# The gate matrix of two feed-forward blocks, by seven products of 2x2 blocks instead of eight

## The chip, the cores and the metric

One NeuronCore of a Trainium2 chip runs the whole program. The metric is the device time of one execution in microseconds (us), the median of several runs. Engines are named as the profile names them: PE is TensorE (PEld its weight loads), DVE is VectorE, ACT is ScalarE, POOL is GpSimd, SP is SyncE, which here only issues DMAs.

## The reference

Two transformer layers over 512 tokens and 1024 features, in fp32. The first has a feed-forward block ahead of its mixer and one behind it, the second has one behind its mixer and its memory attention: three blocks in all, which the kernel numbers f = 0, 1, 2. Each of them computes

```
y = rmsnorm(x, g)                       # 512 x 1024
a = y @ w_gate;  b = y @ w_up           # each 512 x 2816  (in blocks 0 and 1: the halves of one w_in)
x = x + h * ((silu(a) * b) @ w_out)     # h = 0.5 for blocks 0 and 1, 1 for block 2
```

Everything else (sparse attention, convolution, memory attention, gated linear attention) lies between the blocks and is not touched here.

## The kernel before, in words

**Layout.** Features lie on the 128 partitions and tokens along the columns, so an activation is a set of tiles of 128 features x 512 tokens. The 2816 features of `a` and `b` are 22 rows of 128; a block takes them in two halves (h = 0, 1) of 11 (m = 0 to 10), and after each half it multiplies the 11 gated rows by `w_out` (`ffo`) into the residual `XT`.

**fp32 in three passes.** A number is split into a rounded high part and a low part (the rest). Each product is high x high, high x low and low x high, three matmuls that add up in one PSUM bank (`three`, with its matmul at L1135). So one row of `a` (`ffa`) or of `b` (`ffb`) is 8 slices of the 1024 input features x 3 passes = 24 matmuls of 128 x 128 weights on 512 columns (`dense`).

**Weights.** A unit is one row's weights: 128 x 1024 numbers, 512 KB. SP loads it into one of four buffers `raw` as soon as PE has finished the unit four before it; ACT copies it to one of three buffers `whi` as soon as PE has finished the unit three before it (`split` in `act_program`, L1677); DVE subtracts that copy from the raw numbers and writes the low part over them (`split` in `dve_program`, L2115). PE waits for both parts of a unit before its first matmul.

**Order.** There is one list of work items. Every engine walks through it in order and takes the items that concern it, so each engine's program is a fixed sequence, and an instruction that waits holds up all that follow on its engine. The low and high parts of unit u + 2 are put ahead of the DVE and ACT work of the item that uses unit u. In blocks 1 and 2 the list is in the order in which `ffn` writes it:

```
ffa m, ffb m, ffg m,   ffa m+1, ffb m+1, ffg m+1, ...
```

**The gate.** `ffg` of a row is, on DVE: the bank of `ffa` times the row of rsqrt factors `RB` (L2243), a wait for ACT's silu, the bank of `ffb` times `RB` (L2243), the product of the two (L2251), a wait for ACT's copy of the high part, the low part (L2120). The factor 1/rms is applied here, after the matmuls: the operand of the matmuls (`XH`, `XL`) is x times the gain only. The factors come late: `nstat` and `nspread` sum the squares and spread the result over the partitions with PE while PE already works on the first rows, and `RB` is copied out of a bank by DVE (L2223) just before the first `ffg`. In block 2 (f = 2) the first two rows wait for it, in block 1 the first.

**PSUM.** Eight banks; six of them (role `d`) form the ring from which `ffa`, `ffb` and `ffo` take theirs in turn.

Of the kernel before, what the change touches and what calls it, by code (L numbers as in the profile page):

```python
# [310 lines left out]
class Work:  # L311
# [3 lines left out]
    def __init__(self):  # L315
        self.items, self.units, self.heads, self.tiles = [], [], [], []
        self.merged = set()
        self.later = []
        self.spent = 0.0
        self.both = 0  # L320
# [80 lines left out]
def order():  # L401
# [4 lines left out]
    def ffn(f, ni, wa, wb, wo, oa, ob, nxt, jobs):  # L406
        late = []
        for h in range(2):
            for m in range(KF):
                first = h == 0 and m == 0  # L410
                if first and ni in EACH:
                    n, n2 = w.unit(wa, oa), w.unit(wb, ob)
                    w.both = 1
                    w.add_units("pair", (f,), [n, n2])
                    for k in range(KD):
                        w.add("normsq", ni, k)
                    w.both = 0
                    late = [one("ffg", f, h, 0)]
                    continue
# [12 lines left out]
                w.add("ffg", f, h, m)  # L432
                if f == 0 and h == 0 and m == 3:
                    w.add("rel")
                if f == 0 and (m in (4, 7, 10) if h == 0 else m in (1, 4, 7)):
                    w.add("table_out", tables.pop(0))
                if h:
                    w.step(jobs)
            for m in range(KD):
                a = w.unit(wo, h * KD + m, 6 * P)  # L440
                b = w.unit(wo, h * KD + m, 5 * P, 6 * P)
                w.add_units("ffo", (f, h, m), [a, b])
                if f == 0 and h == 0 and m in (2, 5):
# [491 lines left out]
def build(nc, A, out):  # L935
# [158 lines left out]
    full = signal("bank_full")  # L1094
    w_hi, w_lo = signal("weight_hi"), signal("weight_lo")
    x_hi, x_lo = signal("operand_hi"), signal("operand_lo")
# [33 lines left out]
    def pe_program(e):  # L1130
# [162 lines left out]
        def ffo(f, h, m, n, n2):  # L1293
            dense(("ffo", f, h, m), n, GH, GL, ("g", f, h), nk=6, last=False)
            dense(("ffo", f, h, m), n2, GH, GL, ("g", f, h), nk=5, k0=6, first=False)

        def conv(m, part, n):
# [354 lines left out]
        def mmo(m, n, k):  # L1652
# [9 lines left out]
        do = dict(banks=set_banks, nstat=nstat, nspread=nspread, memstat=memstat, warm=warm, start=start, pair=pair, ffa=ffa, ffb=ffb, ffo=ffo, conv=conv,  # L1662
                  convg=convg, wide=wide, widestat=widestat, widefin=widefin, memv=memv, mgate=mgate, score=score,
# [9 lines left out]
    def act_program(e):  # L1673
        on = Once(e)

        def copy(o, i, **how):
            return e.activation(o, i, ACT.Copy, **how)  # L1677

        def split(n):
            width = unit[n][2]  # L1680
            on.wait_ge(*d_raw[n % NRAW].at(n))
            on.wait_ge(*full.at(("u", n - NHI)))
# [68 lines left out]
        def memnorm(i, k):  # L1751
# [4 lines left out]
            if k >= 3:  # L1756
                on.wait_ge(*calc.at(("macc", i, k - 2)))
            e.activation(a[1 + k % 2] if k else a[0], x, ACT.Square).then_inc(*curve.tick(("msq", i, k)))

        def ffg(f, h, m):  # L1760
# [323 lines left out]
        def relload():  # L2084
# [3 lines left out]
        e.dma_start(vec, A["vec"]).then_inc(*d_vec.tick(0, by=16))  # L2088
        do = dict(gain=gain, nspread=nspread, start=start, relload=relload, norm=norm, normsq=normsq, memload=memload, memnorm=memnorm, ffg=ffg, convg=convg,
                  wide=wide, widefin=widefin, memvs=memvs, mgate=mgate, sgate=sgate,  # L2090
# [5 lines left out]
        for (kind, *args), upto in w.items:  # L2096
# [3 lines left out]
            if kind in do:  # L2100
                do[kind](*args)

    def dve_program(e):
        on = Once(e)
        parts = {}

        def split(n):
            name, _, width, _ = unit[n]
            on.wait_ge(*w_hi.at(n))
            if name in STACKED:  # L2110
# [130 lines left out]
        def times(o, item, done, free=True):  # L2241
            on.wait_ge(*full.at(item))
            e.tensor_tensor(o, banks[item], RB, ALU.mult).then_inc(*evac.tick(done, ("free", item)))  # L2243

        def ffg(f, h, m):
            a, s = T[2 * m % 4], T[2 * m % 4 + 1]
            times(a, ("ffa", f, h, m), ("ffat", f, h, m))
            on.wait_ge(*curve.at(("silu", f, h, m)))
# [507 lines left out]
        def final(k):  # L2756
            n = 2 if k < 6 else 1
            if k == 7:
# [7 lines left out]
        e.memset(ZER, 0.0).then_inc(*zeroed.tick("mem"))  # L2766
        do = dict(start=start, norm=norm, normsq=normsq, nstat=nstat, nspread=nspread, memnorm=memnorm, memstat=memstat, ffg=ffg, ffo=ffo, conv=conv, tap=tap, cmerge=cmerge,
                  convg=convg, widestat=widestat, widefin=widefin, memvs=memvs, mgate=mgate, sgate=sgate,
# [61 lines left out]
    def sp_program(e):  # L2830
        on = Once(e)

        def load(n):
            name, j, width, off = unit[n]
            on.wait_ge(*full.at(("u", n - NRAW)))
            if name == "w_gkv":
                h, c = j
                for k in range(2):
                    e.dma_start(raw[n % NRAW].rearrange("p (q k c) -> p q k c", q=4, k=2)[:, :, k, :],
                                A[name][4 * h:4 * h + 4, :, k * 384 + c * P:k * 384 + (c + 1) * P].rearrange("q p c -> p q c")).then_inc(  # L2840
                        *d_raw[n % NRAW].tick(n, by=16))
            else:
                e.dma_start(raw[n % NRAW][:, 0:width], A[name][j, :, off:off + width]).then_inc(*d_raw[n % NRAW].tick(n, by=16))
# [162 lines left out]
```

## Time and profile before

| | |
|---|---|
| Median of 3 runs | 2375.48 us (2374.09 to 2375.69) |
| The profiled execution: its own time | 2373.52 us |
| Its span, first to last instruction | 2371.6 us |
| Granted TensorE clock, mean over the span | 0.999 of full |
| Busy: PE / PEld / DVE / ACT / POOL | 2348.5 / 1966.2 / 1420.3 / 1000.3 / 164.6 us |
| Instructions on PE / DVE / ACT | 11448 / 2891 / 1852 |
| HBM read and written | 217.83 MB and 11.53 MB |

The busy time of an engine is the union of its instructions, so that overlapping matmuls count once. A duration in a row runs from an instruction's start to its recorded end; the next instruction may start a little before that end. In the timeline, "[x <-Y]" behind an instruction says that its engine sat idle for x us before it, until Y was done.

### The profile page before, as it was taken

The page shows a single profiled execution, that of the slowest core. Times are in us where ns is not written, and L with a number is a line of the kernel's source. Part 1 is how long each engine was busy: PE and PEld are TensorE (multiplying, and loading weights), DVE is VectorE, ACT ScalarE, POOL GpSimd, SP SyncE. Part 2 cuts the span into 40 slices and gives each one's busy share as a digit, 9 for nine tenths or more (in the row PEclk, how much of TensorE's full clock was granted, in tenths as well). Part 3 has the DMA queues.
Part 4 walks back from the last instruction along what each step waited for, and adds up shares of the span by engine and source line. Part 5 has one row for each costly group of instructions (what it writes and reads, how often), then busy time and mean ns, then how long its engine had stood idle before and what let it go on. Part 6 is the DMA issues. An engine that isn't in the chain of part 4 may idle for free.

```text
span 2371.6 us, 30179 instructions
## 1 busy us (share of the span) xinstructions
PE 2348.5 (99%) x11448; PEld 1966.2 (83%) x11448; DVE 1420.3 (60%) x2891; ACT 1000.3 (42%) x1852; POOL 164.6 (7%) x250
## 2 busy tenths in 40 slices
PE   9999999999999999999999999999999999999998
PEld 7888889888888888878888888888888887888887
DVE  6434546674658897875434446677754667543444
ACT  5223335442335686653322334666523446322322
POOL 0000000110001223310000000111100001000000
PEclk9999999999999999999999999999999999999999
DMA  4455434332332211223333333212123432223322
GB/s 151 117 119 141 118 112 148 116 107 81 116 102 80 72 54 63 67 90 97 98 90 110 98 108 115 81 55 62 63 80 116 134 106 66 95 89 108 98 88 90
DMA packets 86409, 231.33 MB, mean 98 GB/s; under 512 B 8504, under 2 KB 23480, under 8 KB 86266
## 3 DMA queue, kind: packets, MB, share of 16 engines
q1 hardware_dynamic: 81072, 221.42, 29.4%
q10 hardware_dynamic: 5194, 7.98, 2.1%
q8 instruction: 93, 1.52, 0.3%
q14 instruction: 50, 0.41, 0.1%
HBM read 217.83 MB, written 11.53 MB: 97 GB/s over the span
## 4 chain that ended last, share of the span: by engine, by line
PE 96%; DVE 2%; ACT 1%; issue 1%; POOL 0%; DVEq 0%; ACTq 0%
PE bank L1135 93%; PE bank L1384 2%; PE bank L1210 1%; PE bank L1558 0%; PE bank L1231 0%; DVE t_pw L2387 0%; DVE t_pp L2387 0%; DVE t_PS L2120 0%; DVE t_wlo L2115 0%; ACT t_whi L1677 0%; ACT t_pw L1830 0%; DVE t_XT L2763 0%; DVE t_XL L2124 0%; POOL t_pw L2797 0%; DVE t_PW L2120 0%
## 5 line engine op out<-in xcount | busy, mean ns | idle before, releaser
L1135 PE MATMUL bank<-t_XH,t_whi 128*128 128x512 f32 x2064 | 812.0, 393 | 0.5 <-DVE t_wlo L2115 0.5
L1135 PE MATMUL bank<-t_XL,t_whi 128*128 128x512 f32 x2064 | 803.6, 389 | 0.0
L1135 PE MATMUL bank<-t_XH,t_wlo 128*128 128x512 f32 x2048 | 798.0, 390 | 0.0
L2115 DVE TENSOR_TENSOR t_wlo<-t_raw,t_whi 128x1024 fp32r<-128x1024 f32 (+2 forms) x416 | 478.5, 1152 | 385.8 <-ACT t_whi L1677 382.1
L1677 ACT ACTIVATE t_whi<-t_raw 128x1024 fp32r<-128x1024 f32 (+3 forms) x422 | 416.9, 989 | 436.5 <-PE bank L1135 373.4
L1135 PEld LDWEIGHTS bank<-t_XH,t_whi 128*128 128x128 f32 x2064 | 387.6, 188 | 81.6 <-issue 2.2
L1135 PEld LDWEIGHTS bank<-t_XL,t_whi 128*128 128x128 f32 x2064 | 387.8, 188 | 77.3
L1135 PEld LDWEIGHTS bank<-t_XH,t_wlo 128*128 128x128 f32 x2048 | 384.4, 188 | 81.0
L1135 PE MATMUL bank<-t_RX,t_whi 128*128 128x512 f32 x1056 | 325.1, 389 | 0.0
L2243 DVE TENSOR_TENSOR t_tmp<-bank,t_RB 128x512 f32<-128x512 f32 x178 | 122.5, 688 | 198.3 <-PE bank L1135 193.0
L1135 PEld LDWEIGHTS bank<-t_RX,t_whi 128*128 128x128 f32 x1056 | 198.2, 188 | 41.2
L1135 PE MATMUL bank<-t_RX,t_wlo 128*128 128x512 f32 x528 | 205.4, 389 | 0.0
L1677 ACT ACTIVATE t_RX<-t_tmp 128x512 fp32r<-128x512 f32 x66 | 41.7, 632 | 209.2 <-DVE t_tmp L2251 209.2
L1135 PEld LDWEIGHTS bank<-t_RX,t_wlo 128*128 128x128 f32 x528 | 99.1, 188 | 20.6
L2794 POOL TENSOR_SCALAR t_pp<-t_pp,t_sa,t_gn 128x512 f32<-128x512 f32 (+3 forms) x128 | 88.1, 694 | 335.5 <-DVE t_sa L2400 335.0
L1830 ACT ACTIVATE t_pp<-t_pp,t_sa 128x256 f32<-128x256 f32 (+3 forms) x144 | 79.6, 555 | 52.7 <-DVE t_sa L2387 51.9
L2797 POOL TENSOR_SCALAR t_pw<-t_pw,t_sa,t_cst 128x256 f32<-128x256 f32 (+1 forms) x80 | 47.6, 599 | 726.0 <-DVE t_sa L2400 696.9
L1765 ACT ACTIVATE t_tmp<-t_tmp 128x512 f32<-128x512 f32 x66 | 41.7, 632 | 132.5 <-DVE t_tmp L2243 132.5
L1677 ACT ACTIVATE t_XH<-t_XT,t_vec 128x512 fp32r<-128x512 f32 x48 | 34.5, 724 | 108.1 <-DVE t_XT L2264 52.6
L1135 PE MATMUL bank<-t_OA,t_whi 128*128 128x512 f32 x256 | 79.3, 391 | 0.0
L2264 DVE SCALAR_TENSOR_TENSOR t_XT<-bank,t_XT 128x512 f32<-128x512 f32 x47 | 32.5, 691 | 74.1 <-PE bank L1135 74.1
L2120 DVE TENSOR_TENSOR t_RX<-t_tmp,t_RX 128x512 fp32r<-128x512 f32 x66 | 45.7, 693 | 46.0 <-ACT t_RX L1677 46.0
(334 smaller groups left out, 2678.4 us busy)
## 6 DMA issues: line engine op xcount, KB each, us to landing
t_raw<-in_f_in SPq DMA_DIRECT2D x86, 512.0 KB, 3.5
t_raw<-in_f_out SPq DMA_DIRECT2D x32, 384.0 KB, 3.1
t_raw<-in_w_conv SPq DMA_DIRECT2D x24, 512.0 KB, 3.5
t_raw<-in_w_merge SPq DMA_DIRECT2D x24, 512.0 KB, 3.4
t_raw<-in_fg SPq DMA_DIRECT2D x22, 512.0 KB, 3.4
t_raw<-in_fu SPq DMA_DIRECT2D x22, 512.0 KB, 3.5
t_raw<-in_f_out SPq DMA_DIRECT2D x32, 320.0 KB, 3.0
t_raw<-in_w_g SPq DMA_DIRECT2D x16, 512.0 KB, 3.4
```

The costliest lines, as they stand in the source:

```text
L1135: return e.matmul(o, l, r, start=start, stop=stop, skip_group_check=True)
L1210: f = e.transpose(b[:, i * P:(i + 1) * P], r, ident)
L1384: f = e.transpose(b[:, j * P:(j + 1) * P], spare(hd, t)[:, j * P:(j + 1) * P], ident)
L1677: return e.activation(o, i, ACT.Copy, **how)
L1765: e.activation(s, a, ACT.Silu).then_inc(*curve.tick(("silu", f, h, m)))
L1830: e.activation(p, p, ACT.Exp, scale=-1.0, bias=s[:, 0:1], accum_out=s[:, 1:2]).then_inc(*curve.tick(("ex", t)))
L2115: e.tensor_tensor(wlo[n % NRAW][:, 0:width], raw[n % NRAW][:, 0:width], f32(whi[n % NHI][:, 0:width]), ALU.subtract).then_inc(*w_lo.tick(n))
L2120: e.tensor_tensor(o, x, f32(hi), ALU.subtract).then_inc(*x_lo.tick(item, *more))
L2243: e.tensor_tensor(o, banks[item], RB, ALU.mult).then_inc(*evac.tick(done, ("free", item)))
L2264: e.scalar_tensor_tensor(XT[:, m, :], banks[item], HALF[f], XT[:, m, :], ALU.mult, ALU.add).then_inc(*evac.tick(("free", item), *done))
L2794: e.tensor_scalar(p, p, r, gn[:, i, k:k + 1], ALU.mult, ALU.mult).then_inc(*scaled.tick(t))
L2797: e.tensor_scalar(p, p, r, cst[:, C_ONE:C_ONE + 1], ALU.mult, ALU.mult).then_inc(*scaled.tick(t))
```

## The change

In blocks 1 and 2, 15 of the 22 pairs of neighbouring feature rows of the gate matrix (rows m and m + 1) are computed together. Block 1 keeps its first five rows (`PLAIN`) and the last row of its second half as they were; block 2 keeps its first seven and the same last one. That leaves 3 + 5 pairs in block 1 and 2 + 5 in block 2. `ffb`, the up matrix, stays as it was.

For a pair, two rows x two slices of the input features give a 2 x 2 matrix of weight blocks (128 x 128 each), and the two slices x two halves of the tokens a 2 x 2 matrix of data blocks (128 x 256 each). Their product is formed from seven block products of sums of blocks instead of eight block products. There are four such steps for a pair (q = 0 to 3, two slices each), and the products add up over q in halves of four PSUM banks (`ffs`). Each product still takes three passes, so a pair is 4 x 7 x 3 = 84 matmuls of 256 columns in place of 48 matmuls of 512 columns.

- **Units.** A seven-product unit loads 512 of 1024 columns (256 KB, in runs of 1 KB); `add_up` on DVE forms the four sums of weight blocks beside them (three instructions: 256, 128 and 128 columns, each waiting for the one before). ACT then copies all 1024 columns, and DVE takes their low part, as for any unit.
- **Data.** `xna` on DVE multiplies two slices of x by gain and `RB` (two instructions of 512 columns) and forms four blocks of sums (four of 256); `xnb` splits the seven blocks: three copies on ACT (256, 512 and 1024 columns) and three subtractions on DVE. Four of each per feed-forward block, set between the first items that follow `nspread`.
- **Result.** `ffm` copies one product out on ACT (256 columns) and adds up the seven products on DVE in six instructions (five of 256 columns, one of 512) into the tiles in which `ffg` expects `a`; for these rows `ffg` leaves out its first multiplication by `RB`.
- **Order.** A pair's items are `ffs` q = 0, `ffb` m, `ffs` q = 1, 2, 3, `ffm`, `ffb` m + 1, `ffg` m, `ffg` m + 1: six units, of which four are of the new kind. On DVE, `add_up` of unit n + 1 stands ahead of the low part of unit n.

```
+                seven = f in PLAIN and (m >= PLAIN[f] if h == 0 else m < KF - 1)
+                if seven:
+                    def seven_unit(q):
+                        n = w.unit(wa, (oa + h * KF + m, q), 4 * P)
+                        w.seven.append(n)
+                        w.add_units("ffs", (f, h, m, q), [n])
+
+                    seven_unit(0)
+                    w.lin("ffb", f, h, m, name=wb, j=ob + h * KF + m)
+                    for q in range(1, KD // 2):
+                        seven_unit(q)
+                    w.add("ffm", f, h, m)
+                    w.lin("ffb", f, h, m + 1, name=wb, j=ob + h * KF + m + 1)
+                    w.add("ffg", f, h, m)
+                    w.add("ffg", f, h, m + 1)
+                    m += 2
                     continue
                 w.lin("ffa", f, h, m, name=wa, j=oa + h * KF + m)
...
+                if spread and forms:
+                    w.add(forms[0][0], f, forms.pop(0)[1])
                 w.lin("ffb", f, h, m, name=wb, j=ob + h * KF + m)
                 if first or late:
                     w.add("nspread", ni)
+                    spread = True
+                    if forms:
+                        w.add(forms[0][0], f, forms.pop(0)[1])
                 while late:
                     late.pop()()
...
                 w.add("ffg", f, h, m)
+                if spread and forms:
+                    w.add(forms[0][0], f, forms.pop(0)[1])
```

`forms` is the list xna 0, xna 1, xnb 0, xna 2, xnb 1, xna 3, xnb 2, xnb 3. On the engines, PE, the `split` of ACT, and DVE's walk through the list in turn:

```
+SEVEN = ((A1, X11, 0, 0), (ACD, T2, 0, 1), (AC, T3, 1, 0), (D_, T4, 3, 0), (CD, T1, 3, 1), (B, X21, 2, 0), (ABCD, X22, 2, 1))
...
+        def ffs(f, h, m, q, n):
+            if q == 0:
+                for z in range(4):
+                    take("d", ("ffs", f, h, m, z))
+            hi, lo = weights(n)
+            operand(("xn", f, q))
+            for wi, xi, z, half in SEVEN:
+                o = banks[("ffs", f, h, m, z)][:, 256 * half:256 * half + 256]
+                c, x = slice(wi * P, (wi + 1) * P), slice(256 * xi, 256 * xi + 256)
+                done = three(o, hi[:, c], lo[:, c], NH[q][:, x], NL[q][:, x], q == 0 and wi in (A1, AC, D_, B), q == 3)
...
+            on.wait_ge(*(w_sum if n in summands else d_raw[n % NRAW]).at(n))
...
-        n = 2
+        n, a = 2, 2
         for (kind, *args), upto in w.items:
             while n < min(upto - 1 + NHI, len(unit)):
+                while a < min(n + 2, upto + NHI, len(unit)):
+                    if a in summands:
+                        add_up(a)
+                    a += 1
                 split(n)
                 n += 1
+            while a < min(upto + NHI, len(unit)):
+                if a in summands:
+                    add_up(a)
+                a += 1
```

## Rows read from the trace of the kernel before

**Rows 1.** The page: busy time of each engine; the chain that ended last.
```profile
PE 2348.5 (99%) x11448; PEld 1966.2 (83%) x11448; DVE 1420.3 (60%) x2891; ACT 1000.3 (42%) x1852; POOL 164.6 (7%) x250
...
PE 96%; DVE 2%; ACT 1%; issue 1%; POOL 0%; DVEq 0%; ACTq 0%
```

**Rows 2.** Busy time by window, half 1 of block 1: PE, PEld, DVE, ACT, POOL, clock, DMA.
```profile
1270.00:1379.00 109.00, 109.00 (x482) 90.28 (x481) 51.53 (x62) 32.23 (x40) 0.00 (x0) 1.00 0.29 94
```

**Rows 3.** Timeline of that stretch: start, us, engine, line, operation, tiles.
```profile
1300.60 0.39 PE L1135 MATMUL bank<-t_XH,t_wlo 128*128 128x512 f32 x1
1300.82 0.39 PE L1135 MATMUL bank<-t_XH,t_whi 128*128 128x512 f32 x1
...
1301.01 22.09 SPq L2843 DMA_DIRECT2D t_raw<-in_f_in  x5
1301.08 1.06 ACT L1677 ACTIVATE t_whi<-t_raw 128x1024 fp32r<-128x1024 f32 x1 [2.39 <-PE bank L1135]
1302.17 1.23 DVE L2115 TENSOR_TENSOR t_wlo<-t_raw,t_whi 128x1024 fp32r<-128x1024 f32 x1 [2.23 <-ACT t_whi L1677]
1303.32 0.68 DVE L2243 TENSOR_TENSOR t_tmp<-bank,t_RB 128x512 f32<-128x512 f32 x1
...
1306.53 0.69 DVE L2243 TENSOR_TENSOR t_tmp<-bank,t_RB 128x512 f32<-128x512 f32 x1 [2.53 <-PE bank L1135]
1307.26 0.69 DVE L2251 TENSOR_TENSOR t_tmp<-t_tmp 128x512 f32<-128x512 f32 x1
1308.52 1.05 ACT L1677 ACTIVATE t_whi<-t_raw 128x1024 fp32r<-128x1024 f32 x1
1308.64 0.69 DVE L2120 TENSOR_TENSOR t_RX<-t_tmp,t_RX 128x512 fp32r<-128x512 f32 x1 [0.70 <-ACT t_RX L1677]
```

**Rows 4.** Window of eight slices on 256 columns: matmuls of the memory keys alone.
```profile
368.32:371.19 2.87, 2.87 (x24) 2.82 (x23) 0.00 (x0) 0.00 (x0) 1.00 0.57 153
```

**Rows 5.** Groups of VectorE instructions by shape: count, busy us, mean ns.
```profile
L2251 DVE TENSOR_TENSOR t_tmp<-t_tmp 128x512 f32<-128x512 f32 x66 | 45.7, 692 | 2.2
...
L2124 DVE SCALAR_TENSOR_TENSOR t_XL<-t_XT,t_vec,t_XH 128x512 fp32r<-128x512 f32 x48 | 35.7, 749 | 25.9 <-ACT t_XH L1677 25.5
...
L2120 DVE TENSOR_TENSOR t_PS<-bank,t_PS 128x256 fp32r<-128x256 f32 x32 | 13.3, 416 | 0.8 <-ACT t_PS L1677 0.6
...
L2120 DVE TENSOR_TENSOR t_PS<-bank,t_PS 128x128 fp32r<-128x128 f32 x32 | 9.1, 283 | 1.4 <-ACT t_PS L1677 1.2
```

**Rows 6.** DMA issues: KB each, median us from issue to landing.
```profile
t_raw<-in_f_in SPq DMA_DIRECT2D x86, 512.0 KB, 3.5
...
t_raw<-in_w_gkv SPq DMA_DIRECT2D x24, 256.0 KB, 3.0
...
t_XT<-x_kept SPq DMA_DIRECT2D x16, 256.0 KB, 2.7
...
out<-t_XT SPq DMA_DIRECT2D x8, 256.0 KB, 2.4
```

**Rows 7.** Timeline, start of block 2: VectorE behind the copy of `RB`, then PE.
```profile
2021.21 0.69 DVE L2243 TENSOR_TENSOR t_tmp<-bank,t_RB 128x512 f32<-128x512 f32 x1
...
2025.33 0.68 DVE L2243 TENSOR_TENSOR t_tmp<-bank,t_RB 128x512 f32<-128x512 f32 x1
...
2029.78 2.36 DVE L2115 TENSOR_TENSOR t_wlo<-t_raw,t_whi 128x1024 fp32r<-128x1024 f32 x2 [0.26 <-ACT t_whi L1677]
...
2030.97 0.39 PE L1135 MATMUL bank<-t_XH,t_wlo 128*128 128x512 f32 x1
2031.20 0.42 PE L1135 MATMUL bank<-t_XH,t_whi 128*128 128x512 f32 x1
```

**Rows 8.** Timeline of VectorE, start of block 1, behind the copy of `RB`.
```profile
1094.99 0.69 DVE L2243 TENSOR_TENSOR t_tmp<-bank,t_RB 128x512 f32<-128x512 f32 x1
...
1099.45 1.22 DVE L2115 TENSOR_TENSOR t_wlo<-t_raw,t_whi 128x1024 fp32r<-128x1024 f32 x1 [0.26 <-ACT t_whi L1677]
...
1105.25 0.69 DVE L2243 TENSOR_TENSOR t_tmp<-bank,t_RB 128x512 f32<-128x512 f32 x1 [2.53 <-PE bank L1135]
```

More of the change, by code:

```diff
@@ L90 @@
 NRAW = 4
+PLAIN = {1: 5, 2: 7}
+B, A1, D_, AC, CD, ACD, ABCD = 0, 1, 2, 4, 5, 6, 7
+X11, X21, X22, T1, T3, T2, T4 = range(7)
+SEVEN = ((A1, X11, 0, 0), (ACD, T2, 0, 1), (AC, T3, 1, 0), (D_, T4, 3, 0), (CD, T1, 3, 1), (B, X21, 2, 0), (ABCD, X22, 2, 1))
 class Signal:
@@ L317, in __init__ @@
         self.merged = set()
+        self.seven = []
         self.later = []
@@ L407, in ffn @@
         late = []
+        forms = [("xna", 0), ("xna", 1), ("xnb", 0), ("xna", 2), ("xnb", 1), ("xna", 3), ("xnb", 2), ("xnb", 3)] if f in PLAIN else []
+        spread = False
         for h in range(2):
-            for m in range(KF):
+            m = 0
+            while m < KF:
                 first = h == 0 and m == 0
@@ L432, in ffn @@
                 w.add("ffg", f, h, m)
+                if spread and forms:
+                    w.add(forms[0][0], f, forms.pop(0)[1])
+                    if h == 0 and f in PLAIN and m == PLAIN[f] - 1:
+                        while forms:
+                            w.add(forms[0][0], f, forms.pop(0)[1])
                 if f == 0 and h == 0 and m == 3:
@@ L1029, in build @@
     OM = [place(f"OM{q}", 12800 + q * 1024, 1024, F32R).rearrange("p (k n) -> p k n", k=2) for q in range(2)]
+    NAT = (17920, 21504, 25088, 3072)
+    NS = [place(f"ns{j}", NAT[j], 1792) for j in range(4)]
+    NL = [place(f"nl{j}", NAT[j], 1792, F32R) for j in range(4)]
+    NH = [place(f"nh{j}", NAT[j] + 1792, 1792, F32R) for j in range(4)]
+    TN = [[place(f"tn{d}{q}", (256, 1792)[d] + 512 * q, 512) for q in range(2)] for d in range(2)]
+    P1, U2, V2 = place("p1", 1280, 256), place("u2", 1536, 256), place("v2", 28672, 256)
     sa = [sb(f"sa{i}", [P, 8]) for i in range(RING)]
@@ L1660, in mmo @@
                 banks.let_go(("mmo", m))
-        do = dict(banks=set_banks, nstat=nstat, nspread=nspread, memstat=memstat, warm=warm, start=start, pair=pair, ffa=ffa, ffb=ffb, ffo=ffo, conv=conv,
+        do = dict(banks=set_banks, nstat=nstat, nspread=nspread, memstat=memstat, warm=warm, start=start, pair=pair, ffa=ffa, ffb=ffb, ffs=ffs, ffo=ffo, conv=conv,
                   convg=convg, wide=wide, widestat=widestat, widefin=widefin, memv=memv, mgate=mgate, score=score,
@@ L1679, in split @@
         def split(n):
-            width = unit[n][2]
-            on.wait_ge(*d_raw[n % NRAW].at(n))
+            width = UNIT if n in summands else unit[n][2]
+            on.wait_ge(*(w_sum if n in summands else d_raw[n % NRAW]).at(n))
             on.wait_ge(*full.at(("u", n - NHI)))
@@ L1758, in memnorm, with xnb, ffm @@
             e.activation(a[1 + k % 2] if k else a[0], x, ACT.Square).then_inc(*curve.tick(("msq", i, k)))
+        def xnb(f, j):
+            b, a = TN[j % 2]
+            on.wait_ge(*calc.at(("xn", f, j)))
+            copy(NH[j][:, 0:256], b[:, 0:256]).then_inc(*x_hi.tick(("xn0", f, j)))
+            copy(NH[j][:, 256:768], a).then_inc(*x_hi.tick(("xn0", f, j)))
+            on.wait_ge(*calc.at(("xns", f, j)))
+            copy(NH[j][:, 768:1792], NS[j][:, 768:1792]).then_inc(*x_hi.tick(("xn", f, j)))
+        def ffm(f, h, m):
+            on.wait_ge(*full.at(("ffs", f, h, m)))
+            if merged:
+                on.wait_ge(*evac.at(("ffat", *merged.pop())))
+            merged.append((f, h, m))
+            copy(P1, banks[("ffs", f, h, m, 0)][:, 0:256]).then_inc(*copied.tick(("p1", f, h, m)))
         def ffg(f, h, m):
@@ L2101, in act_program @@
                 do[kind](*args)
+    summands = set(w.seven)
     def dve_program(e):
@@ L2105, in dve_program @@
         parts = {}
+        sevens = set()
         def split(n):
             name, _, width, _ = unit[n]
+            width = UNIT if n in summands else width
             on.wait_ge(*w_hi.at(n))
@@ L2245, in ffg @@
         def ffg(f, h, m):
             a, s = T[2 * m % 4], T[2 * m % 4 + 1]
-            times(a, ("ffa", f, h, m), ("ffat", f, h, m))
+            if (f, h, m) not in sevens:
+                times(a, ("ffa", f, h, m), ("ffat", f, h, m))
             on.wait_ge(*curve.at(("silu", f, h, m)))
@@ L2841, in load @@
                         *d_raw[n % NRAW].tick(n, by=16))
+            elif n in summands:
+                row, q = j
+                e.dma_start(raw[n % NRAW][:, 0:width].rearrange("p (m c) -> p m c", m=2),
+                            A[name][row:row + 2, :, 256 * q:256 * q + 256].rearrange("m p c -> p m c")).then_inc(*d_raw[n % NRAW].tick(n, by=16))
             else:
```

58 lines of the change are left out of this document (54 added, 4 removed).

## The prediction

> **What bounds the kernel now.** Read the page first: PE is busy for 2348.5 of 2371.6 us, and the chain that ended last lies on it for 96% [rows 1]. Both say that only what shortens PE's own work, or makes PE wait, shows in the time. Then take the stage that is changed, by window: in the second half of block 1 PE has no gap in 109 us, while VectorE works for 51.5 and ScalarE for 32.2 [rows 2]. So in these stages whatever PE saves comes off the time as long as the weights arrive, and VectorE has some half of its time to give. Whether that is enough cannot be seen from the sum, since VectorE's order is fixed: the timeline is needed.
>
> In the timeline look at the clockwork of a unit. SyncE's five loads start 22.09 us apart from first start to last end; less one issue of 0.33 this makes four steps of 5.44 us [rows 3], one unit on PE: 24 matmuls, 0.227 us each. PE's end of a unit (its last matmul 1300.60 to 1300.99, the next unit's first at 1300.82) releases the load 0.19 us, and ScalarE 0.26 us, after that next unit has begun [rows 3]; VectorE I put at 0.27. A finished instruction releases another engine about 0.03 us later (ScalarE's copy ends at 1302.14, VectorE starts at 1302.17) [rows 3].
>
> **PE's own saving.** Memory keys show the new shape: three passes on 256 columns, 24 matmuls in 2.87 us, 0.1196 us each [rows 4]. That is more than half of 0.227, so seven products for eight do not save an eighth. A new unit has 7 x 3 = 21 matmuls, 2.51 us. A pair with its two up rows takes 2 x 5.44 + 4 x 2.51 = 20.92 us in place of 4 x 5.44 = 21.76: 0.84 us less, and 15 x 0.84 = 12.6 us if nothing waits.
>
> **VectorE's new work.** Prices: 128, 256 and 512 columns cost 283, 416 and 692 ns, two-step instructions of 512 columns 749 [rows 5]; 1024 columns 1.23 us, and the next independent instruction starts 1.15 us after it, 0.08 before its end, a dependent one 0.03 to 0.04 behind the end (1306.53 + 0.69, next 1307.26) [rows 3]. None of the sums is in the trace with its broadcast operand; I take the rows of the same width; for one of 256 columns the rows of 128 and 512 are the bounds, 0.28 and 0.69.
> - Sum step of a unit: 0.42 + 0.28 + 0.28 and two hand-offs, 0.97 us until the next may start.
> - Low part of a unit: 1.15.
> - Merge of a pair: five of 256 and one of 512 columns, two of them dependent: 2.41.
> - Gate of a row without its first multiplication: 0.73 + 0.72, ScalarE's copy with its hand-offs 0.70 [rows 3], then 0.61 to 0.65: 2.73. With the first multiplication and the wait for silu: 4.12 (2021.21 to 2025.33) [rows 7].
> - Data, first step: two of 749 and four of 256 columns: 2.90. Second step, with ScalarE's copies done: 256, 512 and 1024 columns, 2.10.
>
> Per pair this is 4 x 0.97 + 6 x 1.15 + 2.41 + 2 x 2.73 = 18.7 of PE's 20.9 us. It fits only if VectorE hardly ever waits.
>
> **Where VectorE waits.** Number a pair's units 0 to 5 (0, 2, 3, 4 are new, 1 and 5 the up rows), the next pair's from 6. VectorE's order around unit 5 is: sum of 6, low of 5, low of 6, merge, sum of 8, low of 7, two gates, sum of 9, low of 8. The sum of 6 waits for a load that SyncE starts when PE has finished unit 2, and the low part of unit 5 is queued behind it, though its own numbers are there. From PE's end of unit 2: 0.19 to the issue, the load's landing L, 0.03, the sum 0.97, the low part 1.23, and 0.19 to the first matmul (a low part that ended at 2031.01 met a matmul at 2031.20, so at most that) [rows 7]: L + 2.61. PE reaches unit 5 after two units, 5.02 us. So PE waits L - 2.41, and each pair that is followed by another gains 0.84 - (L - 2.41) = 3.25 - L.
>
> L is not shown for 256 KB in runs of 1 KB. The rows of that size: output stores 2.4, the spilled residual read back 2.7, a gated-attention weight in shorter runs 3.0; a full unit 3.5 [rows 6]. I take 3.0, the row nearest in kind (a strided weight load into the same buffers); bounds 2.4 and 3.5. Gain 0.25 each. There are 2 + 4 in block 1 and 1 + 4 in block 2: 11 x 0.25 = 2.75 us, between 9.2 (no wait) and -2.75. The last pair of each half has no such sum behind it and keeps 0.84: 4 x 0.84 = 3.36. Together 6.1 us.
>
> Is VectorE then on time for unit 8? From the sum of 6: 2.16 (low of 5; low of 6 waits for ScalarE) + 1.15 + 2.41 + 0.97 + 1.15 + 5.46 + 0.97 + 1.42 = 15.69 us. PE from the same point: 2.39 + 5.44 + 2.51 + 5.44 = 15.78. A draw; I count nothing, but any excess is paid on 11 pairs.
>
> **What the data steps cost.** They hide in VectorE's free time between plain rows only as long as a low part behind them is still early.
> - Block 2: before, the first low part behind the two late gates started at 2029.78, 0.33 us after VectorE was free (2025.33 + 4.12 = 2029.45), ended at 2031.01, and PE took it at 2031.20 without a break [rows 7]: no slack. Two first steps now stand ahead of it, one before the gates and one behind: 2 x 2.90 - 0.33 = 5.47 us of PE waiting.
> - Block 1: one late gate. The low part started at 1099.45, 0.34 after VectorE was free (1094.99 + 4.12). It now starts at 1099.11 + 5.80 = 1104.91 and frees PE at 1106.33; PE wants it at 1105.25 - 0.27 = 1104.98 [rows 8]. 1.35 us.
> - Then each pair of plain units carries a first and a second step: 1.15 + 2.10 + 1.15 + 4.12 + 2.90 = 11.42 us of VectorE for PE's 10.88. 0.54 us, twice in each block: 2.16.
> - Block 1 goes into its pairs with one plain row in between, VectorE still behind: the last second step, waiting 0.2 us for ScalarE, and the first sums cost 11.77 - 10.88 = 0.89 and 8.34 - 7.95 = 0.39: 1.28. Block 2 has two plain rows, enough to catch up.
>
> Sum 5.47 + 1.35 + 2.16 + 1.28 = 10.3 us. If the steps were hidden in full it would be 0; if every one of the eight were paid in both blocks, 2 x 4 x (2.90 + 2.10) = 40.
>
> **The sum.** 10.3 - 6.1 = 4.2 us slower. The profiled execution took 2373.5, which gives 2377.7; the median of the runs is 2.0 above it, so 2379.7 is forecast. ScalarE's added copies (some 9 of 21 us per pair in all) lie under VectorE's. Between L = 2.7 and 3.3 the forecast runs from 2376.4 to 2383.0.
>
> **Rivals.**
> 1. *VectorE becomes the bound of the pairs.* For it: the draw above, and that 18.7 of 20.9 us leave no room. Against: the low parts overlap by 0.08 us today [rows 3]. If the thirteen independent starts in the 15.69 us came only at the end of the one before, the chain grows by 1.04, PE waits 0.95 more per pair: 11 x 0.95 = 10.5, 2390. It decides from an excess of 0.1 us. The Trainium skill ("VectorE: DVE Perf Modes", section "The DRAIN you can't avoid") says that the next operation does not start until the pipe is empty. By that rule this rival holds; the trace agrees with it only for dependent instructions (1307.26) and shows 0.08 us of overlap for independent ones (1303.32).
> 2. *The load lands early, not slower.* At L = 2.4 the sum of 6 makes PE wait for nothing, 15 x 0.84 - 10.3 = 2.3 us faster, 2373.2; it is faster than before from L = 2.6 down. For it: stores of this size at 2.4. Against: no load from memory is under 2.7 [rows 6], and a full unit is in flight when this one starts.
> 3. *The data steps hide after all*, because the rows of the steps are shorter than I priced them or PE's wait there eats later slack: 6.1 us faster, 2369.4. Against: block 2's low part had no slack [rows 7], and nothing in VectorE's order can pass it.
> 4. *The change does not give PE its saving:* with four banks in turn, a matmul takes as long as its weight load, 24 loads of some 0.19 (188 to 192 ns) instead of 0.12. 84 x 0.19 = 16.0 for 10.0: 15 x 6.0 = 90 us slower, 2465 less what VectorE then no longer costs. Against: the loads overlap in the window of 256 columns [rows 4].
>
> **How the numbers follow.** Forecast 0.48, rivals 0.22, 0.18, 0.08, 0.04. About 0.2% (4.75 us) can be told from no change: faster is below 2370.7, slower above 2380.2. Of the forecast's 0.48, 2380.2 cuts off some 0.22; with rivals 1 and 4, slower 0.48. Same: the rest, 0.26, with 0.16 of rival 2: 0.42. Faster: 0.08 and 0.02. The range 2371 to 2391 leaves out rival 3, rival 4 and the end of rival 1, 0.18.
>
> **What would show it.** Windows in the pairs: 84 matmuls in 10.0 us. The chain and PE's waits: a wait of about 0.6 us for the low part at each unit 5, 11 times, with VectorE idle ahead of the sum of 6 until a load lands; one wait of some 5.5 us at the start of block 2 and one of 1.4 in block 1. Wrong would be: waits at unit 8 instead (rival 1), a landing of 2.4 (rival 2), no wait at block 2's start (rival 3), PE's steps of 0.19 us (rival 4).

## The result, and the profile after

The change makes the kernel slightly slower: 2381.66 us (median of 10 runs, 2379.03 to 2383.80) against 2375.35 (10 runs, 2374.09 to 2375.80). The ratio is 1.0027, 95% interval 1.0018 to 1.0035. The forecast was 2379.7, the range 2371 to 2391. The profiled execution took 2383.09 us (span 2381.3), near the top of its runs.

The page of the kernel after, which answers to [rows 1]: busy time by engine, and the chain.

```profile
PE 2345.0 (98%) x11988; PEld 1985.0 (83%) x11988; DVE 1561.5 (66%) x3233; ACT 1050.7 (44%) x1921; POOL 166.6 (7%) x250
...
PE 92%; DVE 5%; DMA 1%; ACT 1%; issue 1%; POOL 0%; DVEq 0%; SPq 0%; ACTq 0%
```

PE is busy for 3.5 us less, but VectorE and DMA now hold 6% of the chain, where VectorE held 2%: PE waits. The window of block 1's second half, against [rows 2], shows little of it there: VectorE's work has grown from 51.53 to 84.79 us, PE's idle time is 0.2 us. Idle time understates a wait: it is counted from the recorded end of PE's last matmul, which lies behind the start that the next one would have had. By the loads (below) the waits in this window come to some 1 us.

```profile
1270.00:1379.00 109.00, 108.79 (x664) 97.37 (x664) 84.79 (x145) 45.09 (x55) 0.00 (x0) 1.00 0.32 102
```

PE's waits by window (total, times, longest), first in block 1, then in block 2, show where it is:

```profile
PE bank L1178 <- DVE t_wlo L2190: 4.0, 6, 1.2
...
PE bank L1178 <- DVE t_wlo L2190: 8.9, 8, 5.3
```

All are waits for a low part. The longest, 5.3 us, is at the start of block 2. The timeline of VectorE there answers to [rows 7]:

```profile
2023.36 1.42 DVE L2336 SCALAR_TENSOR_TENSOR t_tn<-t_XT,t_vec,t_RB 128x512 f32<-128x512 f32 x2
...
2026.28 0.68 DVE L2318 TENSOR_TENSOR t_tmp<-bank,t_RB 128x512 f32<-128x512 f32 x1
...
2034.49 1.41 DVE L2336 SCALAR_TENSOR_TENSOR t_tn<-t_XT,t_vec,t_RB 128x512 f32<-128x512 f32 x2
...
2037.41 1.22 DVE L2190 TENSOR_TENSOR t_wlo<-t_raw,t_whi 128x1024 fp32r<-128x1024 f32 x1
```

```profile
2033.11 0.39 PE L1178 MATMUL bank<-t_XH,t_wlo 128*128 128x512 f32 x1
...
2038.77 0.77 PE L1178 MATMUL bank<-t_XH,t_whi 128*128 128x512 f32 x1 [5.27 <-DVE t_wlo L2190]
2039.33 0.63 PE L1178 MATMUL bank<-t_XL,t_whi 128*128 128x512 f32 x1
2039.76 0.63 PE L1178 MATMUL bank<-t_XH,t_wlo 128*128 128x512 f32 x1
```

The first data step takes 2026.28 - 2023.36 = 2.92 us and stands once ahead of the two gates and once (2034.49 to 2037.41) behind them; the low part that PE needs comes last. What PE does behind the gap is new: its matmuls start 0.43 us apart, not 0.23. The windows of that stretch (PE, PEld, DVE, ACT, POOL, granted clock, DMA share, GB/s) say why:

```profile
2028.00:2033.40 5.40, 5.40 (x25) 4.22 (x23) 3.72 (x6) 1.44 (x3) 0.00 (x0) 1.00 0.29 97
2033.50:2038.70 5.20, 0.00 (x0) 0.00 (x0) 4.75 (x9) 4.02 (x6) 0.00 (x0) 0.92 0.32 102
2038.70:2041.00 2.30, 2.23 (x5) 1.84 (x6) 2.30 (x4) 0.00 (x0) 0.00 (x0) 0.50 0.00 0
...
2043.00:2045.00 2.00, 2.00 (x6) 1.59 (x6) 1.38 (x2) 0.52 (x2) 0.00 (x0) 0.57 0.00 0
2045.00:2048.00 3.00, 3.00 (x14) 2.44 (x14) 2.71 (x6) 3.00 (x6) 0.00 (x0) 1.00 0.00 0
```

The granted clock is 1.00 (2.4 GHz) before the gap, 0.50 (1.2 GHz) for some 6 us behind it, and then 1.00 again. What gap and clock cost together is seen in two of SyncE's loads, each of which starts when PE ends a unit. They are 5.50 us apart before and 13.80 after, so 8.3 us are lost here:

```profile
2031.39 0.33 SPq L2843 DMA_DIRECT2D t_raw<-in_fu  x1
2036.89 0.33 SPq L2843 DMA_DIRECT2D t_raw<-in_fg  x1
```

```profile
2033.53 0.33 SPq L2980 DMA_DIRECT2D t_raw<-in_fu  x1
2047.33 0.33 SPq L2980 DMA_DIRECT2D t_raw<-in_fg  x1
```

Inside the pairs, too, the clockwork is best read from SyncE's loads, since a load starts when PE ends the unit four places earlier. From the first of the three loads of units 8 to 10 (one line, x3) to the load of unit 11 PE works on units 5, 6 and 7; without a wait that step takes 13.45 us, as e8 below shows. Second half of block 2:

```profile
2199.09 0.37 SPq L2977 DMA_DIRECT2D t_raw<-in_fg  x1
2201.61 0.34 SPq L2980 DMA_DIRECT2D t_raw<-in_fu  x1
2204.13 9.04 SPq L2977 DMA_DIRECT2D t_raw<-in_fg  x3
2218.27 0.34 SPq L2980 DMA_DIRECT2D t_raw<-in_fu  x1
```

```profile
2202.17 0.43 DVE L2324 TENSOR_TENSOR t_raw<-t_raw 128x256 f32<-128x256 f32 x1 [3.21 <-DMA t_raw<-in_fg]
...
2203.17 2.43 DVE L2190 TENSOR_TENSOR t_wlo<-t_raw,t_whi 128x1024 fp32r<-128x1024 f32 x2
```

The load of unit 6 starts at 2199.09; VectorE idles for 3.21 us until it lands, sums from 2202.17, and only then makes unit 5's low part. The step is 2218.27 - 2204.13 = 14.14: a wait of 0.69. Such steps stand at all 11 places; what they exceed 13.45 by is 0.17 to 1.08, 6.7 us in all. (The expectations of e1 and e5 count 7.7 for the same waits; by these steps it is 6.7.)

For each kernel below, the same four times were read from its profiled execution: the start of block 1's first load, from there to the first load behind block 1, from there to block 2's fifth load (its first four start well ahead of it, between the blocks), and from there to the end of the span.

| kernel | start | block 1 | between | block 2 | median, us | before, us |
|---|---|---|---|---|---|---|
| before | 1066.2 | 365.4 | 576.5 | 363.6 | | |
| after | 1067.5 | 366.3 | 576.4 | 371.1 | 2381.7 | 2375.4 |
| steps alone (e4) | 1068.2 | 367.8 | 576.2 | 371.1 | 2385.2 | 2375.0 |
| steps later (e2) | 1067.4 | 365.5 | 576.2 | 365.8 | 2376.9 | 2375.0 |
| filler (e3) | 1068.6 | 365.6 | 576.2 | 366.2 | 2377.5 | 2375.0 |
| every sum behind (e1) | 1068.7 | 373.2 | 576.2 | 373.3 | 2393.2 | 2375.0 |
| first sum behind (e5) | 1067.5 | 364.7 | 576.2 | 368.1 | 2380.1 | 2374.8 |
| first sum, steps later (e6) | 1068.0 | 368.6 | 576.3 | 365.2 | 2377.9 | 2374.8 |
| sums on GpSimd (e7) | 1069.4 | 363.8 | 576.6 | 366.8 | 2377.6 | 2374.8 |
| sums and subtractions on GpSimd (e8) | 1068.1 | 359.3 | 576.5 | 358.4 | 2364.5 | 2374.8 |
| 13 pairs (e9) | 1067.7 | 362.8 | 578.9 | 362.0 | 2374.2 | 2375.0 |
| sums on GpSimd, steps later (e10) | 1067.9 | 363.8 | 576.5 | 363.2 | 2373.5 | 2375.0 |

The start differs by up to 3 us ahead of any changed code, and e9 lost 2.4 us between the blocks in a wait that no edit touches; so the columns of the blocks say more of an edit than single times do.

### The profile page after: what moved, and what is told of

Read it like the earlier page. It is cut to its first block, busy times and chain, and to the rows that moved or that the text cites. A ratio compares the mean times of both kernels' runs of the same rounds, so it can differ in the third digit from the quotient of the medians.

```text
span 2381.3 us, 31773 instructions
## 1 busy us (share of the span) xinstructions
PE 2345.0 (98%) x11988; PEld 1985.0 (83%) x11988; DVE 1561.5 (66%) x3233; ACT 1050.7 (44%) x1921; POOL 166.6 (7%) x250
## 4 chain that ended last, share of the span: by engine, by line
PE 92%; DVE 5%; DMA 1%; ACT 1%; issue 1%; POOL 0%; DVEq 0%; SPq 0%; ACTq 0%
PE bank L1178 88%; PE bank L1439 2%; DVE t_wlo L2190 1%; DMA t_raw<-in_fg 1%; PE bank L1253 1%; DVE t_tmp L2318 0%; DVE t_tn L2336 0%; DMA t_raw<-in_f_in 0%; PE bank L1613 0%; DVE t_tmp L2376 0%; DMA t_XT<-in_xT 0%; PE bank L1274 0%; DVE t_nl L2195 0%; ACT t_RX L1733 0%; DVE t_pp L2512 0%
## 5 line engine op out<-in xcount | busy, mean ns | idle before, releaser
L1178 PE MATMUL bank<-t_XH,t_whi 128*128 128x512 f32 x1824 | 721.7, 396 | 12.4 <-DVE t_wlo L2190 11.3
L1178 PE MATMUL bank<-t_XL,t_whi 128*128 128x512 f32 x1824 | 711.8, 390 | 0.0
L1178 PE MATMUL bank<-t_XH,t_wlo 128*128 128x512 f32 x1808 | 705.8, 390 | 0.0
L1178 PEld LDWEIGHTS bank<-t_XH,t_whi 128*128 128x128 f32 x1824 | 343.4, 188 | 86.2 <-issue 15.8
L1178 PEld LDWEIGHTS bank<-t_XH,t_wlo 128*128 128x128 f32 x1808 | 340.1, 188 | 72.6
L1178 PEld LDWEIGHTS bank<-t_XL,t_whi 128*128 128x128 f32 x1824 | 343.7, 188 | 67.2
L1178 PE MATMUL bank<-t_nh,t_whi 128*128 128x256 f32 x420 | 119.0, 283 | 1.6 <-DVE t_wlo L2190 1.5
L1178 PE MATMUL bank<-t_nl,t_whi 128*128 128x256 f32 x420 | 118.8, 283 | 0.0
L1178 PE MATMUL bank<-t_nh,t_wlo 128*128 128x256 f32 x420 | 118.8, 283 | 0.0
L1178 PEld LDWEIGHTS bank<-t_nh,t_whi 128*128 128x128 f32 x420 | 80.5, 192 | 4.0 <-ACT t_whi L1733 1.8
```

The costliest lines, as they stand in the source:

```text
L1178: return e.matmul(o, l, r, start=start, stop=stop, skip_group_check=True)
```

## The experiments

**The start of block 2: steps alone, steps later, filler.** Is it the data steps that cost, and is the slow clock the gap's doing?

> The data steps alone, at the places of the kernel after; all 22 pairs of rows computed as before, so the forms that the steps make are read by nobody. Theory: 5.4 + 2.6 us at block 2's start, 1.2 at block 1's, 0.54 twice in block 1: 2375.4 + 10.3 = 2385.7 us. Rival (the steps hide, the loss is in the pairs): 2375.4 us. If the clock at block 2's start stays at 1.00: 2375.4 + 5.4 + 1.2 + 2.2 = 2384.2 us.

```
-                seven = f in PLAIN and (m >= PLAIN[f] if h == 0 else m < KF - 1)
+                seven = False
```

Measured: 2385.16 us, ratio 1.0043 (1.0030 to 1.0055). Block 1 is 2.4 us longer than before, block 2 7.5, together 9.9; the gap at block 2's start is the same 5.26 us. The steps by themselves cost nearly what was expected, without a pair in the kernel; the rival falls. The clock's part was smaller than expected: the step around the gap is 12.96 us here, 13.80 after.

> The kernel after, with the data steps moved: in block 2 none beside the two late gates, the first one a row later and then as before, two to a row, up to the last plain row; in block 1 none ahead of the late gate. The same work on every engine. Theory (the steps cost where a low part behind them has no slack, and block 2's gap of 5.3 us takes the clock down after it): block 2 gets back 5.4 us of waiting and 2.6 us of slow matmuls, block 1 some 2.5 us of waits; 2381.7 - 10.5 = 2371.2 us, with a granted clock of 1.00 at the start of block 2. Rival (the steps hide, the whole loss is in the pairs): 2381.7 us.

```
-                if spread and forms:
+                if spread and forms and m >= f:
...
                     spread = True
-                    if forms:
-                        w.add(forms[0][0], f, forms.pop(0)[1])
...
-                if spread and forms:
+                if spread and forms and m >= 3 * f - 3:
```

(The first place is between a row's two units, the second ahead of the late gates, the third behind a row's gate; the step that reuses a buffer also waits for VectorE's own last reading of it.) Measured: 2376.89 us, ratio 1.0009 (1.0000 to 1.0018): 4.8 us back, where 10.5 were expected. The waits at both starts are gone, but PE now waits where each block goes into its pairs. SyncE's loads there in block 2:

```profile
2070.76 10.22 SPq L2975 DMA_DIRECT2D t_raw<-in_fg  x3
2088.10 0.34 SPq L2978 DMA_DIRECT2D t_raw<-in_fu  x1
```

The step is 17.34 us where 13.42 is the time without a wait: 3.9 us, and 3.8 at the same place in block 1. The waits listed there are of 1.7 and 1.6 us, for gates and for the last data step. VectorE has just as much to do before the first pair as it had; moved later, the work is paid later.

> The kernel after, with 20 matmuls of 512 columns, whose result nobody reads, put on TensorE into the gap at block 2's start: 20 x 0.227 = 4.5 us in a gap of 5.3. VectorE's wait stays where it is. Theory (the gap lets the clock fall): the granted clock stays at 1.00 behind the gap, 2.6 us come back, and of the two waits of 0.54 us that the slow stretch had covered up to 1.1 us show again: 2379.1 to 2380.2 us. Rival (the clock falls for another reason): 0.5 behind the gap as before, 2381.7 us.

```
+                if (f, h, m) == (2, 0, 3):
+                    w.add("warm", 20)
                 w.lin("ffa", f, h, m, name=wa, j=oa + h * KF + m)
```

Measured: 2377.49 us, ratio 1.0010 (1.0001 to 1.0019). The windows of the stretch that had the slow clock:

```profile
2033.50:2038.70 5.20, 4.67 (x21) 3.54 (x19) 4.61 (x9) 4.17 (x6) 0.00 (x0) 1.00 0.31 102
2038.70:2041.00 2.30, 2.09 (x9) 1.77 (x10) 2.30 (x5) 0.00 (x0) 0.00 (x0) 1.00 0.00 0
```

VectorE is as late as before, PE does idle work in the gap, and the clock stays at 1.00. The step between the two loads around the gap (2033.67 and 2044.66 here) falls from 13.80 to 10.99 us: the slow clock had cost 2.8. Two later steps of 5.91 and 5.94 in place of 5.44 show the two waits of 0.5 that the slow stretch had covered. The kernel gained more than these account for (4.2 us): in this execution the waits at unit 5 in block 2's second half are 0.16 to 0.23 us each, against 0.56 to 1.03 after. The pairs are the same code; the loads of 256 KB landed sooner in that half (median 2.6 us, against 2.8; it is 2.6 in e2 too, which has no filler). Landing differs from execution to execution, and with it the pairs. Whether the filler has a part in it stays open.

**The order in the pairs: every sum behind, first sum behind.** Is it VectorE's order at unit 5, or its amount of work?

> The kernel after, but VectorE's sum of the next pair's first unit (unit 6) stands behind the low part of unit 5, no longer ahead of it. The same work on every engine. Theory (a sum that waits for its load holds back a finished low part): the 11 waits at unit 5, 7.7 us in all in the profiled execution after (mean 0.7), go; 2381.7 - 7.7 = 2374.0 us, and a pair followed by another lasts 20.9 us. Rival (VectorE's work fills the pairs): the order changes nothing or costs, since each sum now meets ScalarE's copy at once (0.25 us on 11 pairs): 2381.7 to 2384.4 us.

```
-                while a < min(n + 2, upto + NHI, len(unit)):
+                while a < min(n + 1, upto + NHI, len(unit)):
```

Measured: 2393.19 us, ratio 1.0074 (1.0060 to 1.0087), 11.5 us slower than after: both expectations miss. The edit moved not only the first sum but all. VectorE in one pair, second half of block 2, and SyncE's loads:

```profile
2226.16 1.22 DVE L2190 TENSOR_TENSOR t_wlo<-t_raw,t_whi 128x1024 fp32r<-128x1024 f32 x1 [1.13 <-ACT t_whi L1733]
2227.30 0.42 DVE L2324 TENSOR_TENSOR t_raw<-t_raw 128x256 f32<-128x256 f32 x1
...
2229.50 2.36 DVE L2190 TENSOR_TENSOR t_wlo<-t_raw,t_whi 128x1024 fp32r<-128x1024 f32 x2 [1.12 <-ACT t_whi L1733]
```

```profile
2226.97 0.37 SPq L2977 DMA_DIRECT2D t_raw<-in_fg  x1
2230.31 0.34 SPq L2980 DMA_DIRECT2D t_raw<-in_fu  x1
2233.65 8.35 SPq L2977 DMA_DIRECT2D t_raw<-in_fg  x3
2247.10 0.34 SPq L2980 DMA_DIRECT2D t_raw<-in_fu  x1
```

Unit 5's wait is gone (2247.10 - 2233.65 = 13.45). But sum, ScalarE's copy and low part now follow one another, 2229.50 - 2226.16 = 3.34 us a unit, and PE's new units take 2.52: two waits of up to 0.82 in most pairs. Computing a sum one unit ahead is what hides ScalarE's copy.

> The kernel after, with only the sum of a pair's first unit (unit 6 as counted from the pair before, 11 times) behind the low part of unit 5; the other sums stay one unit ahead, so the chain of sum, copy and low part that cost 3.34 us a unit in the first attempt cannot form. Theory: the waits at unit 5 go, 7.7 us in the profiled execution after and 4.3 in that of the kernel with the filler, where loads landed sooner: 2381.7 - 6 = 2375.7 us (2374.0 to 2377.4), a pair followed by another 20.9 us. Rival (VectorE's work fills the pairs): the idle 1.1 us between that sum and its low part is paid by PE at unit 8, so no gain, 2381.7 us or more.

```
+    heads = {n for n in w.seven if unit[n][1][1] == 0 and n - 4 in w.seven}
...
-                while a < min(n + 2, upto + NHI, len(unit)):
+                while a < min(n + 2 - (n + 1 in heads), upto + NHI, len(unit)):
```

Measured: 2380.14 us, ratio 1.0025 (1.0016 to 1.0035); by the profiled executions the blocks are 1.6 and 3.0 us shorter than after, by the medians the gain is 1.5. All steps over units 5, 6 and 7 are 13.45 but some of the next ones are long:

```profile
2200.75 8.35 SPq L2978 DMA_DIRECT2D t_raw<-in_fg  x3
2214.19 0.34 SPq L2981 DMA_DIRECT2D t_raw<-in_fu  x1
2217.43 0.37 SPq L2978 DMA_DIRECT2D t_raw<-in_fg  x1
```

2217.43 - 2214.19 = 3.24 in place of 2.52: a wait of 0.72 at unit 8, and 0.04 to 0.76 at the others. So the theory holds for unit 5, and the rival's place is right too: behind the late load VectorE has a chain up to unit 8 with no room in it. The first wait had hidden the second.

**VectorE's time: both edits, GpSimd, fewer pairs.**

> Both at once: that order of the first sum, and the data steps moved as in the kernel with later steps. Theory (the two costs are separate): 2376.9 - 6 + 0.5 = 2371.4 us, the two waits of 1.6 to 1.7 us where each block goes into its pairs remaining. Rival (VectorE is short of time over the whole block, so what one edit frees the other takes): 2375 to 2377 us.

The edit joins two of the diffs above, that of the later steps and that of the first sum. Measured: 2377.86 us, ratio 1.0013 (1.0004 to 1.0022), no better than with only the steps moved (2376.89). In the profiled execution the step on block 1's way into the pairs is 5.5 us too long: waits of 1.8 and 1.6 us, and a clock of 0.50 behind them that cost some 1.7. The later steps had 3.8 there without it. The gain at unit 5 did not outweigh this and the waits at unit 8; the rival's time came, by more than its reason.

> The kernel after, with the three sums of each weight unit on GpSimd (0.74 us for 256 columns by its rows, an estimated 0.45 for 128), the rest unchanged. GpSimd is the one that waits for the load then. Theory (VectorE's wait in order, not the amount of its work, makes PE wait in the pairs): waits at unit 5 go, a pair followed by another 20.9 us, 2381.7 - 6 - 1 = 2374.7 us; the wait and the clock at block 2's start stay. Rival 1 (VectorE slows while GpSimd works beside it): low parts longer than 1.23 us and no gain. Rival 2 (the sums come too late from GpSimd): waits of PE for the copies of ScalarE.

The edit moves the function that sums a unit's weights, unchanged, into GpSimd's program, with a loop that runs it for every unit that is three ahead:

```
+            while a < min(upto + NHI, len(unit)):
+                if a in summands:
+                    add_up(a)
+                a += 1
```

Measured: 2377.58 us, ratio 1.0013 (1.0004 to 1.0021). In the second half of block 1 the steps over units 5 to 7 are 13.45 and the next ones 2.52 to 2.68: no engine with other work waits for the load, and PE waits for nearly nothing. The sign of the first rival is there all the same: in the two blocks 50 low parts that overlap an instruction of GpSimd take 1.38 us in the mean and up to 1.76, the 68 others 1.22; in the pairs PE hardly waits for it. The gap of 5.27 us at block 2's start is still there. Expected were 2374.7; the data steps' cost stayed, and in block 1 it grew (a step there of 7.00 us was 5.91 after).

> The sums of the weight units on GpSimd and the data steps at the later places, their subtractions on VectorE: 15 pairs. Theory (VectorE is about 3 us short between the late gates and the first pair, and the first five sums that go to GpSimd give it 4.8 there): no waits where the blocks go into the pairs, 2374.8 - 15 x 0.76 = 2363.4 us, up to 2365. Rival (the four subtractions of each data step are what is too much): 1 to 3 us of waits stay in each block, 2365.5 to 2369.5 us.

The edit joins this loop on GpSimd and the diff of the later steps. Measured: 2373.48 us, ratio 0.9994 (0.9986 to 1.0003). The rival is nearer, though the time lies above its range too: the step on the way into the pairs is 3.8 us too long in both blocks. PE's longest waits there are 2.0 and 1.3 us in block 1, and 2.0 in block 2, where the clock falls behind so short a gap too:

```profile
2077.00:2078.14 1.14, 0.00 (x1) 0.03 (x1) 1.14 (x3) 0.91 (x1) 0.00 (x0) 1.00 0.65 212
...
2079.00:2080.00 1.00, 1.00 (x6) 1.00 (x6) 1.00 (x2) 0.00 (x0) 1.00 (x1) 0.50 0.00 0
...
2083.00:2084.00 1.00, 1.00 (x6) 0.82 (x5) 0.97 (x2) 0.00 (x0) 0.00 (x0) 1.00 0.36 119
```

Why VectorE is late although GpSimd took the sums has a new reason; VectorE and GpSimd just before, in the timeline:

```profile
2060.72 1.03 DVE L2337 TENSOR_TENSOR t_nl<-t_tn,t_nh 128x256 fp32r<-128x256 f32 x2
2061.66 1.76 DVE L2193 TENSOR_TENSOR t_nl<-t_ns,t_nh 128x1024 fp32r<-128x1024 f32 x1
2063.35 1.48 DVE L2188 TENSOR_TENSOR t_wlo<-t_raw,t_whi 128x1024 fp32r<-128x1024 f32 x1
```

```profile
2061.54 0.81 POOL L2902 TENSOR_TENSOR t_raw<-t_raw 128x256 f32<-128x256 f32 x1 [76.59 <-DMA t_raw<-in_fg]
2062.43 1.32 POOL L2905 TENSOR_TENSOR t_raw<-t_raw 128x128 f32<-128x128 f32 x1
2063.83 1.31 POOL L2907 TENSOR_TENSOR t_raw<-t_raw 128x128 f32<-128x128 f32 x1
```

Instructions of 1024 columns that take 1.22 us alone take 1.76 and 1.48 beside GpSimd's, whose 128 columns take 1.32 in place of 0.46 (alone, in e8). Six of VectorE's instructions or pairs of them between 2060.7 and 2077.6 are longer than alone, some 2.0 us in all, as much as PE's wait of 2.00 that follows. That this alone makes VectorE late is argued; no run of its own isolated it. That the instructions are longer beside GpSimd holds over both blocks of this run: 49 low parts that overlap an instruction of GpSimd take 1.41 us in the mean and up to 1.77, the 68 others 1.22 and at most 1.23. The Trainium skill ("SBUF — State Buffer", section "SBUF: two separate sides") says that a VectorE instruction with two inputs in SBUF and a GpSimd instruction that reads SBUF exclude each other at a shared port. The rows agree, and VectorE's multiplications that read a bank take 0.68 us beside GpSimd and 0.69 without.

> The sums of each weight unit and the four subtractions of each data step on GpSimd, and the data steps at the later places. Theory (all of the loss was VectorE's order and time; PE's saving of 0.84 us a pair is real): 2375.3 - 12.6 = 2362.7 us, with up to 1.5 us left where steps meet gates: 2362.7 to 2364.2 us. Rival (PE's saving is smaller than 0.84, or GpSimd slows VectorE): above 2368 us.

The edit adds to the last one that the four subtractions of a data step leave VectorE's program for GpSimd's, with a signal of its own:

```
+        def xna(f, j):
+            b, a = TN[j % 2]
+            on.wait_ge(*calc.at(("xn", f, j)))
+            e.tensor_tensor(NS[j][:, 768:1024], b[:, 256:512], b[:, 0:256], ALU.subtract).then_inc(*w_sum.tick(("xn1", f, j)))
...
```

Measured: 2364.52 us, ratio 0.9962 (0.9949 to 0.9976): faster than both kernels, 10.3 us below before. No wait of PE is listed in either block; the loads in the second half of block 2, against those after:

```profile
2188.20 8.35 SPq L2974 DMA_DIRECT2D t_raw<-in_fg  x3
2201.64 0.34 SPq L2977 DMA_DIRECT2D t_raw<-in_fu  x1
...
2209.20 8.36 SPq L2974 DMA_DIRECT2D t_raw<-in_fg  x3
```

A pair takes 2209.20 - 2188.20 = 21.00 us, 0.76 less than before's 21.76. Block 1 is 6.1 us shorter than before with 8 pairs, block 2 5.2 with 7: 11.3 us by the profile. So PE's saving is real, and nothing but VectorE's order and time had kept it back. Against e10 only the subtractions were moved, and the waits on the way into the pairs went with them.

> VectorE alone again (nothing on GpSimd), with the order of the first sum and the later data steps, and with two more plain rows ahead of the pairs in each block: 13 pairs in place of 15. Theory (where a block goes into its pairs PE waits because VectorE is some 3 us short of time there): the waits of 1.8 and 1.6 us in each block go; of the 9 waits at unit 8 some 0.35 us each stay; 2374.8 - 13 x 0.76 + 3.2 = 2368.1 us. Rival (those waits come from the change of the loop itself, whatever VectorE has behind it): they stay, 2368.1 + 6.8 = 2374.9 us.

The edit is that of e6 and this:

```
-PLAIN = {1: 5, 2: 7}
+PLAIN = {1: 7, 2: 9}
```

Measured: 2374.24 us, ratio 0.9998 (0.9989 to 1.0007): no difference from before. The waits of 1.8 and 1.6 us on the way into the pairs are gone (both steps 13.42), as the theory had it. The blocks are 2.6 and 1.6 us shorter than before, 4.3 together, where 6.7 were expected: ahead of that step 0.7 us are still lost in block 1 and 0.9 in block 2, and waits at unit 8 stay, 3.8 us in all and up to 1.5 each. The median shows still less than the profiled execution; the runs lie between 2371.7 and 2377.3, and what sets them apart was not found.

## Why the prediction came out near, and where its steps were off

The forecast was +4.2 us; the medians say +6.3, the profiled execution +9.6, of which 1.3 arose before block 1. In the blocks the profiled execution lost 0.9 + 7.5 = 8.4, twice the forecast.

- **PE's saving**, put at 0.84 us a pair and 12.6 in all, is 0.76 and 11.4 (e8). The matmuls have the assumed pace (a new unit 2.52 us, against 2.51); the rest of the difference, 0.06, sits in the step over units 5 to 7, 13.45 in place of 13.39. Rival 4 is refuted.
- **The wait at unit 5** came at all 11 places, through the order that the step names. From issue to sum it is 2.6 to 3.5 us, 3.0 in the mean, the L that was taken from the strided weight load [rows 6]. (The prediction's list of rows of that size is not complete: a table read back took 3.8, and the program's first four weight loads 4.5.) The step gives 11 x 0.59 = 6.5 us; measured 6.7. Rival 2 needed L = 2.4; no load of a new unit landed in less than 2.5. That single loads differ by 0.9 us, and the mean of the 11 from one execution to another (2.8 in e3), was not in the estimate.
- **The data steps**, put at 10.3 us, cost 9.9 when they were put in alone (e4). There block 1 is exact in the sum: 1.35 + 2 x 0.54 = 2.43, measured 2.4. Block 2's start is not. The wait was right (5.47; with the filler, e3, the step around the gap is 5.5 us longer than before). But the sum stopped at the gap: the clock fell behind it, for which the prediction has no term, and took 2.8 us more, which in turn covered two waits put at 0.54 each. Rival 3 is refuted.
- **The draw at unit 8.** Rival 1 did not come, except for one wait of 0.9 us in block 2's first half and one of 0.3 in block 1's second. Counting it a draw was fair: once unit 5's wait is taken away, PE waits at unit 8 instead (e5). What the forecast called 9.2 us without a wait at unit 5 was reached by none of the orders tried with the sums on VectorE (e1, e5, e9). Had every start on VectorE waited for the end of the one before, waits would, by rival 1's sum, have stood at unit 8 already after. The Trainium skill ("VectorE: DVE Perf Modes", section "The DRAIN you can't avoid") says that the next operation does not start until the pipe is empty, and also, which the prediction left out, that one that is not held starts earlier. The trace agrees with the addition: an independent instruction starts 1.14 us behind a low part of 1.22.

So the terms are -11.4 + 6.7 + 13.1 = 8.4, against -12.6 + 6.5 + 10.3. The 13.1 are 8.3 at block 2's start, 0.9 and 0.3 at those two units 8, and 3.6 for the data steps in block 1 (3.7 predicted). The step that failed is the cost of the gap in block 2, mis-sized by the clock. This clock cost is itself not a constant: around the same gap of 5.3 us the step was 12.55 (e1), 12.96 (e4), 13.12 (e5), 13.19 (e7) and 13.80 us (after), against 10.99 with the filler, so the slow clock took 1.6 to 2.8, and most in the execution on which this account rests.

All these errors make the change look better than it is. That the medians still came out only 2 us above the forecast is partly luck. Of the 3.3 us between +9.6 and +6.3, 1.8 are that the profiled execution of before lies below its median, and 1.4 that after's lies above its own. What makes after's other executions shorter was not profiled; loads that land sooner, as in e3, and a cheaper gap, as in e1 and e4, would both do it.

## What to carry to other kernels

Where one engine feeds the bound one in a fixed order, look not at its share of busy time but at each instruction that waits for a transfer: what is queued behind it waits too, and may already be due. Taking such a wait away by reordering shows the next one in the chain; here, moving the sums and the subtractions to an idle engine and the data steps to later places removed all of them, and the 15 pairs then gave their 11 us. The sums alone were not enough (e7). And when a gap of several microseconds on TensorE is priced, add what the clock takes after it.

## What the runs showed of the hardware

- A gap of 5.3 us on TensorE, with a granted clock of 1.00 before it, was followed by a stretch at 0.50: some 6 us in after (2.8 us lost), 3.4 in e1 (1.6 lost), between these in e4, e5 and e7. Idle matmuls in the gap kept 1.00 (e3). A gap of 2.0 us brought the clock down in block 2 of e10 and not in block 1. So the price of a gap is not fixed by its length.
- A load of 256 KB in runs of 1 KB landed in 2.54 to 4.61 us in blocks 1 and 2 of after (median 2.8), one of 512 KB in 3.05 to 4.43 (median 3.2): half the bytes saved 0.4 us.
- VectorE and GpSimd slow each other when both read SBUF (e7, e8, e10): in e10 VectorE's 1.22 us became 1.41 in the mean and up to 1.77, and GpSimd's 0.46 became 0.96 in the mean and up to 1.4.
